# Reordering the mixer of a two-stack transformer block: the gated-linear branch first, attention and the convolution's taps behind it

## The reference, cut to what matters

```python
def _context_mixer(h, p):
    proj = h @ p['w_in']
    k, v, kg, vg, gf, gb = _mem_parts(proj[..., :MEM_COLS], p)
    q, qg, r, glu, gates = _rest_parts(proj[..., MEM_COLS:], p)
    o_att = _sdpa(q, k, v)
    o_gla, s_f, s_b = _gla_bidir(qg, kg, vg, gf, gb, zero, zero)
    return _merge(o_att, o_gla, r, glu, gates, p), (k, v, s_f, s_b)
...
def _gla_log_gates(glr, w_a2, b_a):
    z = jnp.einsum('blnr,nrk->nblk', glr.reshape(B, L, 2, GLA_RANK), w_a2) + b_a[:, None, None, :]
    lg = jax.nn.log_sigmoid(z.astype(jnp.float32)) / GLA_TAU
...
def _conv_module(glu, p):
    a, g = jnp.split(glu, 2, axis=-1)
    y = a * jax.nn.sigmoid(g)
    y = lax.conv_general_dilated(y, ...) + p['conv_b_dw']          # depthwise, 31 taps
    y = jax.nn.silu(_layernorm(y, p['conv_ln_g'], p['conv_ln_b']))
    return y @ p['w_conv_o']

def _merge(o_att, o_gla, r, glu, gates, p):
    y_att = o_att... @ p['w_att_o']
    o_gla = _rmsnorm(o_gla, p['gla_norm'])...
    y_gla = (o_gla * jax.nn.silu(r)) @ p['w_gla_o']
    y_conv = _conv_module(glu, p)
    g_att, g_gla, g_conv = jnp.split(jax.nn.sigmoid(gates), N_BRANCH, axis=-1)
    return (g_att * y_att + g_gla * y_gla + g_conv * y_conv) @ p['w_out']
```

## Time and profile before

| | |
|---|---|
| median of 3 runs | 3415.71 us (3413.05 to 3417.04) |
| the profiled execution's own time | 3410.71 us |
| its span | 3408.8 us |
| mean granted TensorE clock | 0.933 |
| mixer 1, from its first matmul behind the norm to the last chunk of h for w_out | 561.50 us |
| mixer 2 | 588.10 us |
| mixer 3 | 556.93 us |

### The profile page before, as it was taken

How to read it: one execution, slowest core, us unless ns; L and a number is a source line. 1 busy time by engine, 2 the same in 40 slices (tenths; PEclk the granted TensorE clock), 3 DMA queues, 4 the chain that set the end, 5 groups by cost and what they waited for, 6 DMA issues and landing times.

```text
span 3408.8 us, 59867 instructions
## 1 busy us (share of the span) xinstructions
PE 2948.4 (86%) x21332; PEld 2714.7 (80%) x21332; DVE 2260.7 (66%) x2987; ACT 1624.1 (48%) x3327; POOL 2413.4 (71%) x2290
## 2 busy tenths in 40 slices
PE   6877969899886898889988868988899889998998
PEld 4766968899875698778987756977799869996898
DVE  4978484676697748477653986494667466646665
ACT  4424544454442555435555424654455445555454
POOL 6958865967793887676874952876778637874687
PEclk6988989999997999989998979999899999998999
DMA  5424422445441443334542421433445314542354
GB/s 192 136 87 149 144 85 87 161 145 171 149 132 61 141 143 106 105 126 136 177 138 73 137 86 50 149 106 109 170 152 178 118 62 147 175 155 80 124 174 166
DMA packets 121577, 441.64 MB, mean 130 GB/s; under 512 B 13552, under 2 KB 15600, under 8 KB 120992
## 3 DMA queue, kind: packets, MB, share of 16 engines
q1 hardware_dynamic: 121088, 435.30, 38.4%
q10 hardware_dynamic: 288, 3.47, 0.3%
HBM read 437.67 MB, written 1.05 MB: 129 GB/s over the span
## 4 chain that ended last, share of the span: by engine, by line
POOL 39%; issue 35%; PE 13%; DVE 10%; ACT 1%; POOLq 1%; DMA 0%; DVEq 0%; SPq 0%; ACTq 0%
POOL w_lo L971 39%; DVE arena L1639 8%; PE lin L451 4%; PE lin L452 3%; PE lin L453 3%; ACT w_hi L1002 1%; POOLq L973 1%; PE aux L583 0%; PE aux L623 0%; POOLq L969 0%; PE lin L479 0%; PE lin L482 0%; PE lin L481 0%; DMA w_raw<-in_stream 0%; DVE arena L1874 0%
## 5 line engine op out<-in xcount | busy, mean ns | idle before, releaser
L971 POOL TENSOR_TENSOR w_lo<-w_raw,w_hi 128x256 fp32r<-128x256 f32 (+1 forms) x2286 | 2413.2, 1087 | 989.0 <-ACT w_hi L1002 986.6
L451 PE MATMUL lin<-h_hi,w_hi 128*128 128x256 f32 x3584 | 1037.3, 289 | 77.4 <-POOL w_lo L971 59.1
L1002 ACT ACTIVATE w_hi<-w_raw 128x512 fp32r<-128x512 f32 x1638 | 937.8, 623 | 246.8 <-PE lin L451 109.5
L452 PE MATMUL lin<-h_lo,w_hi 128*128 128x256 f32 x3584 | 1021.1, 285 | 0.0
L453 PE MATMUL lin<-h_hi,w_lo 128*128 128x256 f32 x3584 | 1020.1, 285 | 0.0
L451 PEld LDWEIGHTS lin<-h_hi,w_hi 128*128 128x128 f32 x3584 | 694.7, 194 | 102.3 <-issue 74.6
L452 PEld LDWEIGHTS lin<-h_lo,w_hi 128*128 128x128 f32 x3584 | 695.2, 194 | 0.6
L453 PEld LDWEIGHTS lin<-h_hi,w_lo 128*128 128x128 f32 x3584 | 694.6, 194 | 0.0
L451 PE MATMUL lin<-s_hi,w_hi 128*128 128x256 f32 x1584 | 463.0, 292 | 44.9 <-issue 20.3
L1639 DVE SCALAR_TENSOR_TENSOR arena<-arena,vec 128x256 f32<-128x256 f32 x720 | 494.1, 758 | 0.0
L452 PE MATMUL lin<-s_lo,w_hi 128*128 128x256 f32 x1584 | 456.0, 288 | 0.0
(11 more groups left out here) (241 smaller groups left out, 4216.2 us busy)
## 6 DMA issues: line engine op xcount, KB each, us to landing
w_raw<-in_stream SPq DMA_DIRECT2D x819, 512.0 KB, 3.3
X<-in_tokens SPq DMA_DIRECT2D x2, 1024.0 KB, 10.4
arena<-in_const ACTq DMA_DIRECT2D x1, 1856.0 KB, 8.2
arena<-in_small ACTq DMA_DIRECT2D x1, 1536.0 KB, 12.7
out<-arena SPq DMA_DIRECT2D x1, 1024.0 KB, 3.9
arena<-in_masks SPq DMA_DIRECT2D x1, 960.0 KB, 11.8
const<-in_const SPq DMA_DIRECT2D x1, 690.0 KB, 7.3
wglr<-in_w_glr SPq DMA_DIRECT2D x1, 384.0 KB, 9.6
```

The costliest lines, as they stand in the source:

```text
L451: used(pe.matmul(o, whi, hi[:, k, :], start=k == 0, stop=False), first)
L452: pe.matmul(o, whi, lo[:, k, :], start=False, stop=False)
L971: ins = pool.tensor_tensor(w_lo[:, slot, part], w_raw[:, slot, part], w_hi[:, slot, part].bitcast(F32), ALU.subtract)
L1002: act.activation(w_hi[:, slot, part], w_raw[:, slot, part], ACT.Copy).then_inc(sems["hi_ready"], 1)
```

## The change

The work is the same, and so are the number of loads (819) and the way they are split; the order within a whole mixer is new. Now it is:
1. kg (4), glr, qg (2), the four gate banks, qg (2); softplus and the prefix sums at once; then the convolution's 16 inputs, with one convolution piece behind each chunk's y but the first (7 pieces); then vg (8 loads).
2. The 17 level steps, filled with r and gg in turn (16 chunks, in all passes) and the ada groups, spread evenly.
3. The O products. O goes to a buffer of its own. Silu of r and Sigmoid of gg are one pass each of ScalarE over 128x2048.
4. K, Q, V, with the norm of O in between (`head256`); VectorE does one convolution piece, then O's s_hi and s_lo, then `inverse`; go 0 follows V, go 1 to 4 stand in the head normalisation.
5. Attention with go 5 to 7, gc (8: the gate of the convolution's branch) and in layer 0 the 8 ada groups as fill; VectorE does 16 convolution pieces in it, behind the units of the same item. Attention's result goes to buffers of its own, a_hi and a_lo.
6. The merge: 8 times g_att and attention's output product, with the convolution's mean behind the first, its variance behind the fourth, its scaling at the fifth, and its s_hi and s_lo in two groups of four at the sixth and seventh; then the convolution's output product (8), with the gate gc made by one Sigmoid of 128x2048, and w_out.

The memory pass interleaves its kt and st units otherwise. arena1 and arena2 become parts of one arena; s_f32 is a float32 view of the bytes of s_hi and s_lo, and r, O and the transposed keys lie in it while s_hi and s_lo are not in use.

The tables, the core of TensorE's and of VectorE's program:

```diff
 
 
+def head_fill():
+
+    return {2: ("go", 1), 4: ("go", 2), 6: ("go", 3), 8: ("go", 4)}
+
+
 def attention_fill(l, s):
 
-    units = [("glr", 0)] + [("vg", c) for c in range(GH)]
+    units = [("go", c) for c in range(5, KC)] + [("gc", c) for c in range(KC)]
     if l == 0:
         units += [("ada", (s, g)) for g in (range(ADA_FIRST, 16) if s == CTX else range(8))]
     return units
@@ -138,9 +143,7 @@
 
 def gla_fill(l, s):
 
-    units = [("cy", c) for c in range(KC)]
-    if s == LAT:
-        units += [("r", c) for c in range(KC)]
+    units = [(kind, c) for c in range(KC) for kind in ("r", "gg")]
     groups = range(16, 20) if s == CTX else range(16, 22) if l else [8, 9, 12, 13, 14, 15]
     units += [("ada", (max(l, s), g)) for g in groups]
...
+MEMORY_UNITS = [("kg", 2), ("kg", 3)] + [("vg", c) for c in range(GH)]
 
 
 def gla_steps(l, s):
 
-    if not whole(l, s):
-        return [[("kg", 2), ("kg", 3)] + [("vg", c) for c in range(GH)]]
-    units = gla_fill(l, s)
-    steps = returned([units[:4], units[4:7]] + spread(units[7:], STEPS - 1))
+    steps = returned(spread(gla_fill(l, s), STEPS))
     if s == CTX:
         for k, u in enumerate(STATE_UNITS):
...
         M = sb("M", [P, KC, S])
-        arena1 = sb("arena1", [P, 10240])
-        arena2 = sb("arena2", [P, 8192])
+
+        with (nc.sbuf_tensor("below_a_hi", [P, 16 * S], F32), nc.sbuf_tensor("a_hi", [P, HEADS, S], F32R) as a_hi,
+              nc.sbuf_tensor("below_a_lo", [P, 8 * S], F32), nc.sbuf_tensor("a_lo", [P, HEADS, S], F32R) as a_lo):
+            pass
+        arena = sb("arena", [P, 74 * S])
+        arena1 = arena[:, 0:40 * S]
+        arena2 = arena[:, 40 * S:72 * S]
...
+                    dense_together(2, ready)
+                    for c in range(2, GH):
+                        dense(h_hi, h_lo)
+                    unit(l, s, ("glr", 0))
+                    low_rank = n.at("lin_done")
+                    for c in range(2):
+                        dense(h_hi, h_lo)
+                    pe.wait_ge(sems["lin_evac"], at.value("lin_evac", low_rank))
+                    gates(l)
+                    for c in range(2, GH):
+                        dense(h_hi, h_lo)
+                    for c in range(2 * KC):
+                        if norm_left and c == 2:
+                            pe.wait_ge(sems["sum_ready"], n.at("sum_ready"))
+                            sum_to_mean()
+                        if norm_left and c == 4:
+                            variance(M)
+                        dense(h_hi, h_lo)
+                    for c in range(GH):
+                        unit(l, s, ("vg", c))
+                    gla(l, s)
+
+                    for c in range(KVH + 2):
+                        dense(h_hi, h_lo)
...
-                    head_rows([("head128", c, hsq[:, c, :]) for _, c in heads])
-                    for c in range(GH if full else 2):
+                    head_rows([("head256", c // 2, gsq[:, c, :]) for c in range(KC)])
+                    for c in range(2, HEADS):
...
+                    token_major()
+                    heads = [(K[:, c, s * S:(s + 1) * S], c) for c in range(KVH)] + [(Q[:, c, :], KVH + c) for c in range(HEADS)]
+                    pe.wait_ge(sems["sq_ready"], at.up("sq_ready"))
+                    head_rows([("head128", c, hsq[c]) for _, c in heads])
+                    n.up("s_ready", KC)
+                    unit(l, s, ("go", 0))
+                    heads_normed(heads, s, head_fill(), lambda u: unit(l, s, u))
...
+                    for c in range(KC):
+                        dense(h_hi, h_lo)
+                        dense(a_hi, a_lo)
+                        if c == 0:
+                            pe.wait_ge(sems["conv_done"], at.up("conv_done"))
+                            for k in range(KC):
+                                mean_chunk(CV, k)
+                        if c == 3:
+                            variance(csq)
...
+                    n.up("lin_evac", GH + 1 + 2 + 4 + 2)
+                    scans()
+                    dve.memset(YP[:, :, 0:PAD], 0.0)
...
+                        if c:
+                            convolve(l, next(pieces), y0)
+                    for c in range(GH):
+                        unit(l, ("vg", c))
+                    gla(l, s)
...
+                    dve.wait_ge(sems["silu_ready"], at.up("silu_ready"))
+                    convolve(l, next(pieces), y0)
...
+                    inverse(aux[0], ROWS, name="row_ready")
+                    dve.wait_ge(sems["silu_ready"], at.up("silu_ready"))
+                    unit(l, ("go", 0))
+                    heads += [(Q[:, c, :], "q_norm") for c in range(HEADS)]
+                    heads_normed(heads, head_fill())
...
+                    fill = returned(spread(attention_fill(l, s), len(items)))
+                    last = spread([("conv", p) for p in pieces], len(items))
+                    attention(items, float(DH) ** -0.5, probs, True, [f + p for f, p in zip(fill, last)], lambda u: unit(l, u, y0))
...
+                        merge_chunk(c, gate_buf[:, c % 2, :])
+                        if c == 0:
+                            centre(CV, CV)
+                        if c == 4:
+                            inverse(aux[1])
+                            dve.wait_ge(sems["xc_ready"], at.now("xc_ready"))
+                            for k in range(KC):
+                                scale_chunk(CV, lambda k: v1(l, "conv_ln_g", k), k, CV)
+                        if c in (5, 6):
+                            for k in range(4 * c - 20, 4 * c - 16):
+                                dve.wait_ge(sems["sigmoid_ready"], at.up("sigmoid_ready"))
+                                y = CV[:, k, :]
+                                step(dve.scalar_tensor_tensor(y, y, v1(l, "conv_ln_b", k), csq[:, k, :], ALU.add, ALU.mult))
+                                both_parts(s_hi[:, k, :], s_lo[:, k, :], y, "s_ready")
+                    dve.wait_ge(sems["silu_ready"], at.up("silu_ready"))
```

More of the change, by code:

```diff
@@ new lines, in program @@
+        gbuf = view(arena, 40 * S, KC, S)
+        probs = view(arena, 48 * S, 2, 2 * S)
+        probsT = view(arena, 52 * S, 2, 2 * QT, P)
+        YP = view(arena, 56 * S, KC, S + 2 * PAD)
+        glr = view(arena, 65 * S, S)
+        CV = view(arena, 66 * S, KC, S)
+        csq = view(arena, 48 * S, KC, S)
+        W = view(arena, 40 * S, KC, S)
+        early = view(arena, 48 * S, KC, S)
+        stage = view(arena, 56 * S, N_MASK, P)
+        assert KC * (S + 2 * PAD) <= 9 * S and N_MASK * P <= 8 * S
@@ new lines, in _ @@
+                    for c in range(GH):
+                        unit(l, ("kg", c))
+                    unit(l, ("glr", 0))
+                    for c in range(2):
+                        unit(l, ("qg", c))
+                    gates(l)
+                    softplus(l, [("qg", 2), ("qg", 3)])
+                    n.up("y_ready", KC)
+                    for c in range(KC):
+                        o = arrived()
+                        moved(act.activation(YP[:, c, PAD:PAD + S], o[:, 0:S], ACT.Copy))
+                        o = arrived()
+                        buffered(c, "y_ready")
+                        moved(act.activation(gate_buf[:, c % 2, :], o[:, 0:S], ACT.Sigmoid))
+                        if norm_left and c == 0:
+                            squares(early, M, "xc_ready")
+                        if norm_left and c == 1:
+                            root(aux[1])
+                        if norm_left and c == 2:
+                            shifted(pl, before, "ln2_b", early)
@@ L1346, in _ @@
                     n.up("sq_ready")
-                    for tt in range(QT):
-                        o = arrived()
-                        moved(act.activation(V[:, s * QT + tt, :], o[:, 0:KVH * DH], ACT.Copy))
-                    if not full:
-                        root(aux[1])
-                        unit(l, ("glr", 0))
-                        shifted(pl, before, "ln2_b", Q)
-                    root(aux[0], ROWS)
-                    for c in range(GH if full else 2):
-                        unit(l, ("kg", c))
@@ L1388, in _ @@
-                    gla(l, s, full)
-                    if not full:
-                        continue
-                    root(aux[0], ROWS)
-                    if s == CTX:
-                        for c in range(KC):
-                            unit(l, ("r", c))
-                    act.wait_ge(sems["lin_evac"], n.at("lin_evac"))
-                    act.activation(rbuf[:, :, :], rbuf[:, :, :], ACT.Silu).then_inc(sems["silu_ready"], 1)
-                    for c in range(KC):
-                        moved(act.activation(gbuf[:, c, :], arrived()[:, 0:S], ACT.Sigmoid))
@@ L1733, in hat_product, with scans @@
                 n.up("hat_ready")
-            def gla(l, s, full):
-                fill = gla_steps(l, s)
-                dve.wait_ge(sems["lin_evac"], at.up("lin_evac", 4))
-                for u in fill[0][:2]:
```

(16 more changed lines are left out.)

773 lines of the change are left out of this document (364 added, 409 removed).

## The result

The changed kernel takes 3442.3 us (median of 4 runs, 3439.32 to 3447.79), the one before 3415.28 (4 runs, 3413.05 to 3417.04): a ratio of 1.0081, 95% interval 1.0064 to 1.0099. It is slower by 27 us; forecast was 3385. The profiled execution took 3443.29 us, the one before 3410.71, so the two profiles lie 32.7 us apart.

A forecast was written before the change was run, and what follows sets the result against it. TensorE, fed by POOL's weight splitting, bounds the kernel, with 294 us of mixer idle reachable by reordering. Mixers -20, -3 and -10, memory pass +2: total -31, span 3378, median 3385 us; own range 3357 to 3407, 8 in 10 3340 to 3440.

The forecast's parts named there:

- The price of attention: Attention of mixers 1, 2, 3: 145, 157 and 132 us, with 160 convolution operations on VectorE where 70 were.
- Today 24 loads ... Four more at 2.9 are 11.6; a third goes into idle time: 107: Mixer 3's level steps: 28 loads instead of 24, so 107 us instead of 99.8.
- The opening: First stage of a mixer, kg to vg, 32 loads: 114 us, with 14 more in mixer 2 for the left-over norm.
- K to the heads: K, Q, V, go 0 and head normalisation: 83 us in the latent pass, 74 in the context pass.
- The merge and what follows: Merge, convolution's output product and products into h at each mixer's end: 95 us.
- The stretch with the memory pass: Memory pass, whose units only change places: 2 us longer.
- The wait for the root: TensorE's wait ahead of the spread rows in head normalisation: falls from 80 us to under 20.
- only moved: Rival: idle time ahead of the heads returns wholly as idle time in attention, no change, 3415 us; chance 0.13.
- The rival on the other side: Attention VectorE-bound with everything colliding, go units' buffers blocking ScalarE: 3408 us from collisions alone, 3444 with both; chance 0.21.
- The lock rule: Rival: in attention a collision costs VectorE 0.72 us instead of 0.45, 56 us more, 3441; chance 0.05.
- More than forecast: Rival: fuller clock and smaller gaps, 12 us less per attention and 3 at each heads stage, 3340 us; chance 0.15.
- Its own signs: Signs: root wait under 20 us, attention 125 to 160, mixer 1 gaining most; wrong if level steps exceed 115.

The follow-up runs named there:

- e4: Kernel before, with only the six convolution pieces ahead of the heads' norm root moved into attention (13 pieces instead of 7): 3407.85 us, ratio 0.9988.
- e2: Changed kernel with only one tap of five done in each of attention's 16 convolution pieces, a bound and no usable version: 3272.63 us, ratio 0.9597.
- e1: Changed kernel with four convolution pieces done right behind the level steps, leaving 12 in attention instead of 16: 3380.26 us, ratio 0.9917 to the kernel before.

## Why the prediction was wrong

**The forecast's direction** was wrong: 31 us faster in the sum, 32.7 slower in the profile. The three mixers took 65 us more than their forecast of 541, 585.5 and 546.5, and half of that (33 us) lies in one step of the sum, the level steps with the O matmuls behind them. Point by point:

*The price of attention was right.* The terms were 145, 157 and 132 us; measured are 145.4, 160.8 and 131.4. The pitch of a convolution operation there (busy time by count) was 0.68, 0.70 and 0.54 us in mixers 1, 2 and 3; the prediction had 0.65 to 0.75.

```profile
L1700 DVE SCALAR_TENSOR_TENSOR arena<-arena,vec 128x256 f32<-128x256 f32 x160 | 109.5, 757 | 0.0
...
L1700 DVE SCALAR_TENSOR_TENSOR arena<-arena,vec 128x256 f32<-128x256 f32 x160 | 111.8, 768 | 0.0
...
L1700 DVE SCALAR_TENSOR_TENSOR arena<-arena,vec 128x256 f32<-128x256 f32 x160 | 85.6, 605 | 0.0
```

*"Today 24 loads ... Four more at 2.9 are 11.6; a third goes into idle time: 107" is the step that failed most.* Level steps and O matmuls were put at 113, 122.5 and 122.5 us and took 124.3, 133.0 and 133.6: 33 of the 65 us.

In mixer 3 the count was wrong. The 24 is POOL's count of the stretch (x95). POOL works ahead of TensorE and, in the O stage behind, splits nothing: part of what it split there was used later. TensorE's own work in that stretch is one chunk of cy, 8 of r and 6 ada groups, 21 loads, so the change adds 7 loads, not 4; its matmuls there went from 608 to 776, which is 7 loads of 24. With 7 loads the prediction's own reckoning gives 99.8 + two thirds of 20.3, 113 us, and the steps took 118.2.

The rest is the overlap, which was put too high. TensorE's idle time in these steps was to take in a third of the new work and fell from 17.2 to 14.4 us only. In mixer 1 this is the whole of it: 12 loads were added (464 matmuls before, 753 now) where 11.5 were counted, TensorE was put at 104 us busy of 105, and it was busy for 98.8 of 112.2. The O matmuls behind took 12.1 us there and not 8. What held the steps was not isolated by a run. The profile shows VectorE waiting for ScalarE's Exp of a step for 22.8 us in 10 times in mixer 3, where it was 7.7 us in 6 times, and ScalarE, which does things in order, waiting for TensorE's banks of r and gg for 31.2 us in 15 times in the same stretch.

*The opening* was put at 114, 128 and 114 and took 119.9, 133.8 and 117.8: 15.5 us. I had let 18 loads meet VectorE's 62 us of convolution at 3.5 us and the other 14 pass at 2.9. But VectorE is busy there for 84.0 us in mixer 3 and 90.6 in mixer 2, with scans, products and the left-over norm. In mixer 3 it first waits 33.5 us for ScalarE's softplus, while POOL splits 32 pieces (8 loads) at 0.70 us each; in the 80 us from 1925.5 on it is busy for 79.8, and POOL splits 88 pieces (22 loads) at 0.89 us. So 22 loads were slowed and not 18.

*The merge and what follows*, put at 95, took 99.4, 99.1 and 97.5: 11 us. *K to the heads*, put at 74, 83 and 83, took 74.3, 84.3 and 84.0. The stretch with the memory pass was to grow by 2 us and is 0.5 shorter (375.3 to 374.8).

*The wait for the root went away*, as forecast, and three idles of 25 us with it. That it would not pay for the longer attention was in the rivals at 13% ("only moved"), and e4 shows that this is what the exchange by itself does: 3408 against 3411. My sum had both sides of it right, three idles of 25 us against 47 + 49 + 50 for attention (149 measured in all), and counted on the other stages to pay the difference, the level steps above all, whose work and idle time it had wrong.

*The rival on the other side* gave 3444 and the result is 3442, but not by its mechanism. It had ScalarE blocked by go units' buffers: in the three attentions the profile has no wait of ScalarE for that product at all, VectorE waits for ScalarE there (18.3 us in 9 times in all). And its further collisions and waits were to lengthen attention, which came out at its forecast length. It was right in one thing: VectorE is the engine waited for. ScalarE does stand blocked behind it in attention, for the softmax's maximum (60.8, 85.6 and 78.5 us in mixers 1, 2 and 3), and in mixer 1 TensorE waits for w_lo for 25.9 us in 11 times there.

*The lock rule* of the Trainium skill ("SBUF — State Buffer", section "SBUF: two separate sides") was to lengthen the three attentions by 56 us. They are 3.6 us longer than the sum by the rows had them. In mixer 2 the 160 operations took 111.8 us: at 0.88 against 0.43 that is 96 collisions with its 108 splitting pieces, a share of 0.89 where I took 0.8. At the rule's 1.15 it would be 60 collisions, so attention alone does not tell the two apart; the stretch in which both engines step along at 0.88 does. The last section shows where one engine was shut out.

*More than forecast* was to come from a better clock. It went the other way: 0.72, 0.81 and 0.79 in attention against 0.86, 0.94 and 0.91. I did not price a worse clock. e2 shows that it came from VectorE's hold on attention. How much of the 27 us the clock costs by itself was not separated.

*Its own signs.* The wait for the root (15.4 us, under 20), attention's length, VectorE's share in it (86 to 89%) and the order of the mixers (1 did best, 2 worst) came out as written, though no mixer gained. TensorE was busy for 88% of mixer 1's level steps and not for over 95%, and mixer 3's steps of 118.2 us lie beyond the 115 that it had named as a sign of being wrong.

## What to carry to other kernels

When an edit moves work from a place where it is waited for into a stage, look first whether the engine that gets it is that stage's longest: in attention every operation moved in (from 7 pieces to 13) or out (from 16 to 12) was worth its full 0.39 to 0.47 us, and nothing was hidden. Look for the engine's idle stretches (28.7 us behind the level steps, some 30 in the steps) and put the work there; 34 operations in the steps cost 0.13 to 0.26 us each. And count the work of a stage by what its consumer does in it, not by what a producer that runs ahead has done in the same window.

## What the runs showed of the hardware that was not expected

The collision of the two engines is not always 0.45 us to one side and 0.15 to the other. In the kernel before, in mixer 3, VectorE ran ten convolution operations back to back at 0.40 us each, about its pitch alone (0.43, rows 5):

```profile
1919.62 4.04 DVE L1639 SCALAR_TENSOR_TENSOR arena<-arena,vec 128x256 f32<-128x256 f32 x10
```

and the splitting piece that POOL had begun meanwhile took 3.80 us instead of 0.72, until VectorE's run was over:

```profile
1920.77 3.80 POOL L971 TENSOR_TENSOR w_lo<-w_raw,w_hi 128x256 fp32r<-128x256 f32 x1 [5.26 <-ACT w_hi L1002]
```

The same was seen at 132.3 us (3.81 us) and at 940.7 us (3.45 us) there, at 976.8 us in the changed kernel (3.45 us), and in e1 behind the level steps (6.06 us, beside 17 operations in a row). Where its wait is shown (5.3 to 17 us), POOL had been idle and came into a run that was under way. There the engine that came second was shut out altogether. The Trainium skill ("SBUF — State Buffer", section "SBUF: two separate sides") has the one that comes second fully blocked while the first holds the shared ports for a whole instruction. The trace agrees in the blocking, but here it lasted through seven instructions in a row or more and not through one. Once both are in step, they advance at 0.88 us. It happens one to three times in an execution (three before, once in the changed kernel, twice in e1) and costs POOL some 3 to 5 us each time; what decides between the two was not tried.
